# First layer of a decoder step on one core: the sample group's values stream past placed probabilities

## The chip, the cores and the metric

The kernel runs on one core of a Trainium2 chip. The metric is the device time of one execution in microseconds (us). The core has a matrix engine (TensorE, PE in the profile; its weight loads are shown apart as PEld), VectorE (DVE), ScalarE (ACT), GpSimd (POOL) and a queue that issues transfers (SyncE, SP). They run at the same time and meet only at semaphores. Matrix products are accumulated in PSUM, which has eight banks of 512 fp32 columns by 128 partitions.

## The reference

One inference step of a two-layer decoder, for a prompt of 512 tokens and for 8 sample sequences of one token each. This is the part that the change touches, cut from the function for the sample group in the first layer:

```python
def dilated_sample(q, k_new, v_new, k_buf, v_buf, rel_bias):
    ...
    for w, d in A_BRANCHES:                       # (128,1), (512,4), (2048,16)
        offs = branch_offsets(w, d)
        idx = wb + j[:, None] - offs[None, :]
        ...
        kg = jnp.where(in_buf, jnp.take(k_buf, ib, axis=1), jnp.take(k_new, inew, axis=1))
        vg = jnp.where(in_buf, jnp.take(v_buf, ib, axis=1), jnp.take(v_new, inew, axis=1))
        o, lse = gathered_attention(q, kg, vg, rel_bias_for(rel_bias, offs, h), (idx >= 0)[None])
    return combine_branches(outs, lses)
```

For each of 8 samples and 8 heads of 64 dimensions, a softmax over 256 cached keys and the new one, and the sum of the 257 value vectors weighted by it. The three branches are folded into one softmax with the logarithm of a count in the bias. Beside it the first layer has the same attention for the prompt, and a gated linear attention (GLA) with a state per sample; their joint result goes through an output projection and a SwiGLU block (called ffn below).

## The kernel before

Everything is fp32 at the borders. The large products are computed as three products of split operands (w_hi with act_hi, w_hi with act_lo, w_lo with act_hi), each of them 128x260 columns in fp32r (L701). ACT rounds a weight block to w_hi (`high`), POOL subtracts to get w_lo (`low`); two blocks are in flight. The input projection of the first layer has 25 such blocks (numbers 0 to 24); block n is written to one of two places in PSUM (banks 0 and 1 for even n, 2 and 3 for odd n) and moved out by ACT, which signals `free_a`. The last block is computed by `last_reader` (L880), which is done with chunks 4 to 7 of act_hi and act_lo first, so that staging for the attention can start in them.

The prompt attention of the first layer has 32 units (4 pairs of heads, 2 heads, 4 blocks of 128 queries, with 128, 256, 384 or 512 keys). It is a software pipeline whose order is written out by hand: step i issues on PE the scores of unit i (three fp32r products, L772), turns the probabilities of unit i-3 (L781) and adds the values of unit i-4 (L793); DVE adds the bias (L1761) and scales (L1769), ACT takes the exponential (L1374) and copies the turned probabilities (L1381). Scores go to banks 0 and 1, turned probabilities to 2 and 3, outputs to 4 and 5.

Behind each step a function `sample_a(i)` puts one piece of the sample group's work, in banks 6 and 7, on each engine's queue. On PE: GLA outputs of the samples (`sample_out_b`, step 0, 16 products of 2 columns, L1066), sum of squares for the last block's head norm (`last_head_sum`, step 1, L717), new values turned to rows (step 3, L1109; DVE copies them to `vnA` at step 4, L2015), norm sums of the GLA output (`norm_b`, 5 times from step 4, L1043), scores of the 8 samples (steps 5 to 15, L1078), probabilities turned (step 21, L1115), the new key's probability taken out (step 23, L1121), values of the 8 samples (steps 26 to 34, L1090) and the new value's share (step 35, L1126).

The values of one sample are 8 products: for each of 4 pairs of heads and 2 blocks of 128 keys, the cached values (128 keys by 128 dimensions) are the stationary operand and the probabilities of the two heads, two columns, move. The queries are laid out sparsely in `qzA` (2048 columns by 128 rows, mostly zero, in yA), which DVE clears (L2000) and fills (L2005) before its first unit. A plain fp32 product takes two records of the trace on PE.

## Time and profile before

| | us |
|---|---|
| median of 3 runs | 1583.71 |
| lowest and highest | 1576.1, 1595.62 |
| the profiled execution | 1597.1 |
| its span | 1595.3 |
| mean granted TensorE clock in it | 0.971 |

The rows further down are of the profiled execution; its span runs from the first to the last instruction, and 1.8 us of its time lie around that. "PEclk" is the share of TensorE's full clock that was granted: 1.00 is 2.4 GHz, 0.50 is 1.2 GHz, and there is nothing between.

### The profile page before, as it was taken

To read this page: it belongs to the slowest core of one execution; us is meant where nothing else is said; L and a number is where in the kernel's file an instruction comes from. 1 tells how busy PE (TensorE), PEld (TensorE's weight loads), DVE (VectorE), ACT (ScalarE), POOL (GpSimd) and SP (SyncE) were. 2 spreads that over 40 slices of the span, in tenths; PEclk is the share of its full clock that TensorE was granted. 3 is DMA by queue.
4 is the path that set the end of the run, shared out by engine and by line. 5 is a ranking of instruction groups with operands and counts; after the bars stand their busy time and mean duration, and the time that the engine had idled before them with its cause. 6 is when DMAs were issued, how large, how long until landed. Compare 5 with 4: busy or idle time off the path is not lost.

```text
span 1595.3 us, 31072 instructions
## 1 busy us (share of the span) xinstructions
PE 1537.8 (96%) x12240; PEld 1482.3 (93%) x12240; DVE 681.6 (43%) x1175; ACT 657.7 (41%) x1094; POOL 684.1 (43%) x350
## 2 busy tenths in 40 slices
PE   7999989999999999999989996999999999999998
PEld 6999967999999999999979785999999999999998
DVE  4044456145444343212341767775634443431224
ACT  4242646224433434222453554664344334332234
POOL 3654752033444444444336464221444444444444
PEclk9999979699999999999989997999999999999999
DMA  4222433122222323323223331121233332233333
GB/s 173 84 101 70 125 124 102 67 80 80 93 92 91 91 84 92 104 92 105 85 77 117 94 90 62 45 81 48 81 91 92 92 92 92 84 100 92 105 92 120
DMA packets 52837, 146.92 MB, mean 92 GB/s; under 512 B 5485, under 2 KB 18057, under 8 KB 52250
## 3 DMA queue, kind: packets, MB, share of 16 engines
q1 hardware_dynamic: 50346, 137.17, 27.7%
q10 hardware_dynamic: 2416, 8.72, 1.5%
q8 instruction: 50, 0.82, 0.2%
q14 instruction: 25, 0.20, 0.0%
HBM read 139.11 MB, written 6.76 MB: 91 GB/s over the span
## 4 chain that ended last, share of the span: by engine, by line
PE 89%; DVE 8%; ACT 2%; issue 1%; DMA 0%; SPq 0%; ACTq 0%; DVEq 0%
PE PS L701 70%; PE PS L793 4%; PE PS L772 3%; DVE act_lo L1741 2%; PE PS L781 2%; PE PS L1090 1%; PE PS L717 1%; PE PS L1078 1%; PE PS L770 1%; DVE top L2094 1%; PE PS L1156 1%; PE PS L1211 1%; DVE pp L1852 0%; DVE xC L2098 0%; PE PS L1066 0%
## 5 line engine op out<-in xcount | busy, mean ns | idle before, releaser
L494 POOL TENSOR_TENSOR w_lo<-w_raw,w_hi 128x1024 fp32r<-128x1024 f32 x217 | 534.9, 2465 | 802.9 <-ACT w_hi L1294 802.9
L701 PE MATMUL PS<-act_hi,w_hi 128*128 128x260 f32 x2576 | 739.4, 287 | 22.5 <-DVE act_lo L1741 12.5
L701 PE MATMUL PS<-act_lo,w_hi 128*128 128x260 f32 x2576 | 731.2, 284 | 0.0
L701 PE MATMUL PS<-act_hi,w_lo 128*128 128x260 f32 x2576 | 730.7, 284 | 0.0
L1294 ACT ACTIVATE w_hi<-w_raw 128x1024 fp32r<-128x1024 f32 x217 | 230.0, 1060 | 713.8 <-PE PS L701 710.0
L701 PEld LDWEIGHTS PS<-act_hi,w_hi 128*128 128x128 f32 x2576 | 488.0, 189 | 36.8 <-issue 23.6
L701 PEld LDWEIGHTS PS<-act_lo,w_hi 128*128 128x128 f32 x2576 | 488.7, 190 | 0.4
L701 PEld LDWEIGHTS PS<-act_hi,w_lo 128*128 128x128 f32 x2576 | 488.7, 190 | 0.0
L701 PE MATMUL PS<-h_hi,w_lo 128*128 128x260 f32 x704 | 198.8, 282 | 0.0
L701 PE MATMUL PS<-h_hi,w_hi 128*128 128x260 f32 x704 | 198.6, 282 | 0.0
L701 PE MATMUL PS<-h_lo,w_hi 128*128 128x260 f32 x704 | 198.5, 282 | 0.0
L701 PEld LDWEIGHTS PS<-h_hi,w_hi 128*128 128x128 f32 x704 | 132.6, 188 | 0.0
L701 PEld LDWEIGHTS PS<-h_lo,w_hi 128*128 128x128 f32 x704 | 132.3, 188 | 0.0
L701 PEld LDWEIGHTS PS<-h_hi,w_lo 128*128 128x128 f32 x704 | 132.2, 188 | 0.0
L1816 DVE TENSOR_TENSOR h_lo<-tmp,h_hi 128x520 f32 x44 | 84.0, 1908 | 40.1 <-ACT h_hi L1432 40.1
L1821 DVE TENSOR_TENSOR x<-PS,x 128x520 f32<-128x520 f32 x16 | 11.2, 699 | 176.5 <-PE PS L701 176.5
L1741 DVE SCALAR_TENSOR_TENSOR act_lo<-x,vecs,act_hi 128x520 fp32r<-128x520 f32 x48 | 70.8, 1494 | 23.2 <-ACT act_hi L1305 23.2
L1808 DVE TENSOR_TENSOR tmp<-PS,sq 128x520 f32<-128x520 f32 x44 | 30.8, 701 | 103.8 <-ACT sq L1428 103.8
L1812 DVE TENSOR_TENSOR tmp<-PS,tmp 128x520 f32<-128x520 f32 x44 | 30.8, 700 | 96.3 <-PE PS L701 96.3
L1381 ACT ACTIVATE tmp<-PS 128x128 f32<-128x128 f32 (+1 forms) x96 | 41.6, 433 | 71.1 <-PE PS L781 69.8
L1732 DVE TENSOR_TENSOR sqsum<-sqsum,sq 128x520 f32<-128x520 f32 x48 | 56.3, 1172 | 21.9 <-ACT sq L1300 21.1
L1806 DVE TENSOR_TENSOR tmp<-PS,nrs 128x520 f32<-128x520 f32 x44 | 30.8, 699 | 68.1 <-PE PS L701 68.1
(332 smaller groups left out, 1824.6 us busy)
## 6 DMA issues: line engine op xcount, KB each, us to landing
w_raw<-in_w SPq DMA_DIRECT2D x217, 512.0 KB, 3.5
kcA<-in_cache_k SPq DMA_DIRECT2D x8, 512.0 KB, 4.3
biasC<-scratch_rows SPq DMA_DIRECT2D x12, 256.0 KB
x<-in_xT SPq DMA_DIRECT2D x4, 520.0 KB, 5.9
out_y<-x SPq DMA_DIRECT2D x8, 260.0 KB, 4.5
vcA<-in_cache_v SPq DMA_DIRECT2D x4, 512.0 KB, 5.5
kcC<-in_pool_k SPq DMA_DIRECT2D x16, 128.0 KB, 2.5
vcC<-in_pool_v SPq DMA_DIRECT2D x16, 128.0 KB, 2.0
```

The costliest lines, as they stand in the source:

```text
L494: pool.tensor_tensor(w_lo[:, s, :], w_raw[:, s, :], w_hi[:, s, :].bitcast(F32), ALU.subtract).then_inc(S("w_lo"), 1)
L701: mm = pe.matmul(PS[:, 2 * place + half, 0:HALF], w[:, s, j * P:(j + 1) * P], r[:, c, cols], start=first and n == 0 and i == 0, stop=last ...
L772: mm = pe.matmul(PS[:, i % 2, 0:W], q_of[part][par][:, p % 2, qb * P:(qb + 1) * P], k[:, k_chunk(p), 0:W], start=n == 0 and not masked, st ...
L781: mm = pe.transpose(PS[:, 2 + i % 2, kb * P:(kb + 1) * P], ps[i % 3][:, kb * P:(kb + 1) * P], ident)
L793: mm = pe.matmul(PS[:, 4 + p % 2, qb * P:(qb + 1) * P], v_of(p, par, kb), pt[:, i % 2, kb * P:(kb + 1) * P], start=i % 8 == 0, stop=i % 8 ...
L1294: act.activation(w_hi[:, s, :], w_raw[:, s, :], ACT.Copy).then_inc(S("w_hi"), 1)
L1381: act.activation(pt[:, i % 2, 0:W], PS[:, 2 + i % 2, 0:W], ACT.Copy).then_inc(S("t_c"), 1)
L1732: dve.tensor_tensor(sqsum[:], sqsum[:], sq[:, m % 2, :], ALU.add).then_inc(S("ssum"), 1)
L1741: dve.scalar_tensor_tensor(act_lo[:, c, :], x[:, c, :], vecs[:, g:g + 1], act_hi[:, c, :].bitcast(F32), ALU.mult, ALU.subtract).then_inc(S ...
L1806: dve.tensor_tensor(halves(tmp[:, 1, :]), slot(0), halves(nrs[:]), ALU.mult).then_inc(S("f_a"), 1)
L1808: dve.tensor_tensor(halves(tmp[:, 1, :]), slot(0), halves(sq[:, 0, :]), ALU.mult).then_inc(S("free_v"), 1)
L1816: dve.tensor_tensor(h_lo[:, bass.ds(f, 1), :], tmp[:, 0:1, :], h_hi[:, bass.ds(f, 1), :].bitcast(F32), ALU.subtract).then_inc(S("h_lo"), 1)
```

## The change

Six edits, in the first layer only.

1. Values of a sample (`sample_values_a`): the turned probabilities are written by ACT into `pzA`, a field of zeros, so that for sample b and key block kb there is a stationary operand of 64 columns (one for each pair of head and sample) in which only the 8 columns of sample b are filled. The cached values of all heads (128 keys by 512) move. All 16 products accumulate in one bank, rows 0 to 63; a 17th product with the new keys' probabilities and values closes the sum. The result holds every head's row against every head's values; DVE copies it to `oA` (step 32), and four products with pieces of the identity (step 33) pick each head's own 64 dimensions and turn them to the layout that the output projection reads. The values stand at steps 24 to 31 instead of 26 to 34.
2. POOL clears `pzA` (128x1032) once the samples' scores are done; ACT waits for it at step 22.
3. DVE clears and fills `qzA` while the last input blocks are computed, before the first unit.
4. The first layer's scores use banks 2 and 3 and its turned probabilities banks 0 and 1, so that the first scores no longer wait for the last block to be moved out.
5. In the last input block ACT rounds the next weights behind the eviction instead of ahead of it, POOL adds the squares' term before its subtraction, and the transfer of the samples' state is issued before the key split. GLA outputs of the samples go half to step 0, half to step 1, the head sum to step 2; the new values are turned in bank 6, which `norm_b(0)` no longer waits for but the first sample scores do.
6. ACT and DVE split the samples' attention output straight from PSUM at the end of the stage, ahead of the last two GLA heads (`high_b`, `low_b` of 1 and 3).

```diff
-        VALUES_A = (26, 27, 28, 29, 30, 32, 33, 34)
+        VALUES_A = tuple(range(24, 32))
+        def score_bank(base, i):
+            return (2 if base == BASE_A else 0) + i % 2
+        def turned_bank(base, i):
+            return (0 if base == BASE_A else 2) + i % 2
...
+                if pair == 2:
+                    pool.wait_ge(S("s_ks"), NS)
+                    pool.memset(pzA, 0.0).then_inc(S("sm_pz"), 1)
...
             def norm_b(h):
                 pe.wait_ge(S("b_sq"), h + 1)
-                if h == 0:
-                    pe.wait_ge(S("sm_pnc"), 1)
-                else:
+                if h:
                     pe.wait_ge(S("b_ln"), h)
...
-            pe.wait_ge(S("free_a"), AB_BLOCKS + 2)
+            pe.wait_ge(S("free_a"), AB_BLOCKS + 1)
...
             def sample_values_a(b):
                 if b == 0:
+                    pe.wait_ge(S("sm_ptc"), 1)
+                    pe.wait_ge(S("b_ln"), 5)
+                pe.wait_ge(S(f"values{b % 6}"), 16 * (b // 6 + 1))
+                for kb in range(2):
+                    c = P * b + 64 * kb
+                    mm = pe.matmul(PS[0:64, 7, :], pzA[:, c:c + 64], value_place(b)[:, kb, :],
+                                   start=b == 0 and kb == 0, stop=False)
+                mm.then_inc(S("s_vs"), 1)
+                if b == NS - 1:
                     pe.wait_ge(S("sm_pnc"), 2)
-                pe.wait_ge(S(f"values{b % 6}"), 16 * (b // 6 + 1))
-                for t in range(4):
-                    for kb in range(2):
-                        c = t * NS + b
-                        mm = pe.matmul(PS[:, 7, 256 + 2 * c:258 + 2 * c], value_place(b)[:, kb, t * P:(t + 1) * P],
-                                       ptsA[:, kb, c:c + 33:32], start=kb == 0, stop=kb == 1)
-                mm.then_inc(S("s_vs"), 1)
+                    pe.matmul(PS[0:64, 7, :], pnA, vnA[:], start=False, stop=True).then_inc(S("sm_o"), 1)
...
-                elif i == 35:
-                    pn = pnA.rearrange("k (r t b) -> k r t b", r=2, t=4)
+                elif i == 33:
+                    pe.wait_ge(S("sm_oc"), 1)
                     for t in range(4):
-                        mm = pe.matmul(PS[:, 6, 16 * t:16 * t + 16], vnA[:, t * P:(t + 1) * P], pn[:, :, t, :],
+                        by_head = ident[0:64, 0:64].rearrange("k (r c) -> k r c", r=2)[:, :, NS * t:NS * t + NS]
+                        mm = pe.matmul(PS[:, 6, 256 + 16 * t:272 + 16 * t], oA[:, t * P:(t + 1) * P], by_head,
                                        start=True, stop=True)
...
                 elif i == 22:
                     act.wait_ge(S("sm_pt"), 1)
-                    act.activation(ptsA, PS[:, 7, 0:P].rearrange("p (n c) -> p n c", n=2),
+                    act.wait_ge(S("sm_pz"), 1)
+                    act.activation(pzA.rearrange("p (b m) -> p b m", b=NS)[:, :, 0:P:NS],
+                                   PS[:, 6, 0:P].rearrange("p (m b) -> p b m", b=NS),
                                    ACT.Copy).then_inc(S("sm_ptc"), 1)
...
             attention(PAIRS_A, BASE_A, xsA, psA3, statA, sample_a)
+            act.wait_ge(S("sm_o"), 2)
+            for r in range(2):
+                rows = slice(HD * r, HD * r + HD)
+                act.activation(act_hi[rows, 0:4, SEQ:NT], sample_out_a(r), ACT.Copy).then_inc(S("sm_oh"), 1)
             act.wait_ge(S("t_s"), 32)
             high_b(1)
             high_b(3)
-            act.wait_ge(S("sm_os"), 2)
-            act.activation(act_hi[:, 0:4, SEQ:NT], osA, ACT.Copy).then_inc(S("sm_oh"), 1)
```

On PE at steps 24 to 28, where the values of samples 0 to 2 stood before (vcA and s are places of cached values, nrs holds the turned probabilities):

```order
L772 MATMUL PS<-act_hi,q_hiA 128x384 [waits t_x]
...
L793 MATMUL PS<-tmp,rs 128x128 x2
L1090 MATMUL PS<-nrs,vcA 128x2 [waits values0,sm_pnc]
L1090 MATMUL PS<-nrs,vcA 128x2 x7
L772 MATMUL PS<-act_hi,q_hiA 128x512 [waits t_x]
...
L1090 MATMUL PS<-nrs,s 128x2 [waits values2]
L1090 MATMUL PS<-nrs,s 128x2 x7
```

And the same engine in the changed kernel, from step 24 and then at its end (yA holds pzA, sqsum the new values):

```order
L808 MATMUL PS<-tmp,rs 128x128 [waits A_st,A_zero,t_c]
L1103 MATMUL PS<-vcA,yA 64x512 [waits values0,b_ln,sm_ptc]
L1103 MATMUL PS<-vcA,yA 64x512
L787 MATMUL PS<-act_hi,q_hiA 128x256 [waits t_x]
...
L1103 MATMUL PS<-s,yA 64x512 [waits values1]
L1103 MATMUL PS<-s,yA 64x512
L1108 MATMUL PS<-sqsum,nrs 64x512 [waits sm_pnc]
...
L1143 MATMUL PS<-const,yA 128x16 [waits sm_oc]
L1143 MATMUL PS<-const,yA 128x16 x3
```

Eight products of 2 columns for each sample have become two of 512 columns, and they begin two steps earlier.

On PE behind the last input block, steps 0 to 5 before:

```order
L772 MATMUL PS<-act_hi,q_hiA 128x128 [waits k_split,A_st,t_x,A_zq,free_a]
...
L1066 MATMUL PS<-qz,s 128x2 [waits A_v,s_new,s_qz]
L1066 MATMUL PS<-qz,s 128x2 x15
...
L717 MATMUL PS<-sq,const 128x260 [waits n_rs,sq_e2,n_e2,hn_ln]
...
L1109 MATMUL PS<-const,yA 8x128 [waits b_o]
...
L1043 MATMUL PS<-s,const 128x512 [waits sm_pnc,b_sq]
...
L1074 MATMUL PS<-sbA 64x257 [waits sm_qz,sm_bias]
```

And now:

```order
L787 MATMUL PS<-act_hi,q_hiA 128x128 [waits k_split,A_st,t_x,A_zq,free_a]
...
L1078 MATMUL PS<-qz,s 128x2 x7
L787 MATMUL PS<-act_hi,q_hiA 128x256 [waits t_x]
...
L1078 MATMUL PS<-qz,s 128x2 x7
...
L732 MATMUL PS<-sq,const 128x260 [waits n_rs,sq_e2,n_e2,hn_ln]
...
L1126 MATMUL PS<-const,yA 8x128 x4
...
L1056 MATMUL PS<-s,const 128x512 [waits b_sq]
...
L1087 MATMUL PS<-sbA 64x257 [waits sm_pnc,sm_qz,sm_bias]
```

The GLA outputs (qz,s) are cut in two with the second unit's scores between them, and the wait for the copy of the new values (sm_pnc) has gone from the norm sum (L1043 before, L1056 now) to the first product of the sample scores.

On ACT around the eviction of the last input block, before:

```order
L1294 ACTIVATE w_hi<-w_raw 128x1024 [waits w_used,w_raw0]
L1533 ACTIVATE q_loA<-const 64x1024 [waits s_kv]
L1545 ACTIVATE act_hi<-yA 128x2x512 [waits act_free,hn_ok]
L1347 ACTIVATE yA<-PS,gains 128x520 [waits w_used]
L1348 ACTIVATE sq<-PS 128x520
L1330 ACTIVATE rs<-PS,vecs 128x520 [waits hn_ok,hn_ss]
```

And now:

```order
L1554 ACTIVATE q_loA<-const 64x1024 [waits s_kv]
L1565 DMA out_s_state<-s 128x2048 [waits s_new]
L1568 ACTIVATE act_hi<-yA 128x2x512 [waits act_free,hn_ok]
L1366 ACTIVATE yA<-PS,gains 128x520 [waits w_used]
L1367 ACTIVATE sq<-PS 128x520
L1311 ACTIVATE w_hi<-w_raw 128x1024 [waits w_used,w_raw0]
```

The rounding of the next weights (w_hi) has moved from the front of this row of work to behind the eviction, and the state's transfer to the front.

## Rows read from the trace of the kernel before

**Rows 1.** The page: busy time of the engines, and the chain that ended last.

```profile
PE 1537.8 (96%) x12240; PEld 1482.3 (93%) x12240; DVE 681.6 (43%) x1175; ACT 657.7 (41%) x1094; POOL 684.1 (43%) x350
...
PE 89%; DVE 8%; ACT 2%; issue 1%; DMA 0%; SPq 0%; ACTq 0%; DVEq 0%
PE PS L701 70%; PE PS L793 4%; PE PS L772 3%; DVE act_lo L1741 2%; PE PS L781 2%; PE PS L1090 1%; PE PS L717 1%; PE PS L1078 1%; PE PS L770 1%; DVE top L2094 1%; PE PS L1156 1%; PE PS L1211 1%; DVE pp L1852 0%; DVE xC L2098 0%; PE PS L1066 0%
```

**Rows 2.** Windows from the last input block to the ffn; PEclk is the granted clock.

```profile
core 0: us, PE busy (x) PEld busy (x) DVE busy (x) ACT busy (x) POOL busy (x), PEclk, DMA share, GB/s
202.00:205.20 3.20, 1.36 (x9) 0.84 (x8) 2.56 (x4) 3.17 (x5) 3.14 (x2) 1.00 0.00 0
205.40:218.80 13.40, 13.19 (x52) 11.99 (x53) 7.68 (x17) 6.14 (x13) 6.08 (x7) 0.50 0.31 117
219.00:222.20 3.20, 0.94 (x9) 0.75 (x7) 3.13 (x9) 1.79 (x7) 3.06 (x5) 1.00 0.21 86
222.50:225.60 3.10, 2.96 (x8) 1.96 (x9) 0.23 (x1) 0.00 (x0) 1.95 (x3) 0.50 0.55 220
225.90:270.00 44.10, 42.30 (x248) 30.81 (x247) 27.63 (x75) 24.94 (x73) 14.68 (x16) 1.00 0.46 144
270.30:273.40 3.10, 3.10 (x14) 3.00 (x14) 1.90 (x10) 1.58 (x4) 0.00 (x0) 0.50 0.02 5
273.70:287.00 13.30, 13.30 (x112) 12.69 (x111) 6.56 (x26) 7.09 (x22) 0.00 (x0) 1.00 0.24 77
287.30:324.60 37.30, 37.30 (x171) 36.55 (x170) 7.96 (x24) 6.71 (x17) 0.00 (x0) 0.50 0.12 43
324.90:340.00 15.10, 15.10 (x128) 15.10 (x127) 6.60 (x5) 3.36 (x5) 4.81 (x2) 1.00 0.27 88
```

**Rows 3.** Windows, PE alone: steps 24 to 35 at either clock.

```profile
core 0: us, PE busy (x), PEclk, DMA share, GB/s
275.50:287.10 11.60, 11.60 (x101) 1.00 0.29 91
287.10:320.10 33.00, 33.00 (x152) 0.50 0.14 49
```

**Rows 4.** Timeline of PE, the value products at either clock, and the end.

```profile
279.11 1.84 PE L1090 MATMUL PS<-nrs,vcA 128*128 128x2 f32 x16
280.82 0.48 PE L772 MATMUL PS<-act_hi,q_hiA 128*128 128x512 f32 x1
...
288.82 3.41 PE L1090 MATMUL PS<-nrs,kcA 128*128 128x2 f32 x16
292.09 0.67 PE L772 MATMUL PS<-act_hi 128*128 128x384 f32 x1
...
318.29 1.89 PE L1126 MATMUL PS<-nrs,sqsum 8*128 8x16 f32 x8
320.10 0.59 PE L701 MATMUL PS<-act_hi,w_hi 128*128 128x260 f32 x1
```

**Rows 5.** Timeline of PE at the full clock: fp32 products of 257 and 512 columns.

```profile
244.63 1.95 PE L1078 MATMUL PS<-kcA,yA 128*64 128x257 f32 x8
246.52 1.12 PE L1043 MATMUL PS<-s,const 128*128 128x512 f32 x2
247.08 0.63 PE L772 MATMUL PS<-act_hi 128*128 128x128 f32 x1
```

**Rows 6.** Timeline of all engines, steps 0 and 1.

```profile
202.62 1.06 ACT L1545 ACTIVATE act_hi<-yA 128x1024 fp32r<-128x1024 f32 x1
...
203.71 1.40 DVE L1965 TENSOR_TENSOR act_lo<-yA,act_hi 128x1024 fp32r<-128x1024 f32 x1 [0.64 <-ACT act_hi L1545]
...
205.03 1.27 DVE L1968 COPY vtokA<-PS 128x512 f32<-128x512 f32 x2
...
205.36 0.44 PE L772 MATMUL PS<-act_hi,q_hiA 128*128 128x128 f32 x1 [1.58 <-DVE act_lo L1965]
...
206.45 6.96 PE L1066 MATMUL PS<-qz,s 128*128 128x2 f32 x32 [0.21 <-DVE vtokA L1968]
206.68 1.76 DVE L2000 MEMSET yA<- 128x2048 f32 x1 [0.38 <-issue]
...
208.48 1.91 DVE L2005 COPY yA<-yA 64x32 f32<-64x32 f32 x2
...
210.43 0.29 DVE L1761 CUSTOM_DVE_ANT_0 xA<-PS,biasA 128x128 f32<-128x128 f32 x1
```

**Rows 7.** Timeline of PE, step 4: the wait ahead of the first norm sum.

```profile
222.64 2.05 PE L1043 MATMUL PS<-s,const 128*128 128x512 f32 x2 [2.70 <-DVE sqsum L2015]
...
226.31 0.64 PE L1074 MATMUL PS<-sbA 33*64 33x257 f32 x2
```

**Rows 8.** Timeline, step 21: the wait ahead of the turned sample probabilities.

```profile
269.93 0.34 PE L1115 MATMUL PS<-const,nrs 64*128 64x64 f32 x2 [1.33 <-DVE nrs L1862]
```

More of the change, by code:

```diff
@@ L539, in body @@
                         finish(n - 1, like - 1)
+                    q = normed(l, n, like)
+                    final = l == 0 and like == AB_BLOCKS - 1
+                    if final:
+                        add_eps(l, q, q % 2, n)
                     low(n + (b0 + 2), (b0 + like) % 2)
@@ L542, in body @@
                         after_low(like)
-                    q = normed(l, n, like)
-                    if q is not None:
+                    if q is not None and not final:
                         add_eps(l, q, q % 2, n)
@@ L1062, in sample_out_b @@
                 pe.wait_ge(S("A_v"), QB)
-                for i in range(2):
-                    for b in range(NS):
-                        c = 2 * (i * NS + b)
-                        mm = pe.matmul(PS[:, 7, c:c + 2], s0[:, b, i, :], qz8[:, i, b, :], start=True, stop=True)
+                for b in range(NS):
+                    c = 2 * (i * NS + b)
+                    mm = pe.matmul(PS[:, 7, c:c + 2], s0[:, b, i, :], qz8[:, i, b, :], start=True, stop=True)
                 mm.then_inc(S("s_o"), 1)
@@ L1335, in body @@
                 def body(n, like):
-                    high(n + (b0 + 2), (b0 + like) % 2)
+                    final = l == 0 and like == AB_BLOCKS - 1
+                    if not final:
+                        high(n + (b0 + 2), (b0 + like) % 2)
                     if before_evict:
@@ L1348, in body @@
                         act.activation(halves(sq[:, s, :]), place, ACT.Square).then_inc(S("free_a"), 1)
+                        if final:
+                            high(n + (b0 + 2), (b0 + like) % 2)
                     elif rank:
@@ L1947, in _ @@
             ins.then_inc(S("s_qz"), 1)
+            qz = qzA.rearrange("p m c -> p (m c)")
+            dve.wait_ge(S("s_qz"), 1)
+            then(dve.memset(qzA, 0.0))
             dve.wait_ge(S("s_in"), 16)
@@ L1960, in _ @@
                                   s0[:, b0:b0 + 4, i, :], ALU.add).then_inc(S("s_new"), 1)
+            dve.wait_ge(S("hn_ok"), 4 + 2)
+            for r in range(2):
+                rows = slice(HD * r, HD * r + HD)
+                dst = qz[rows, 32 * r:32 * r + 31 * 65 + 1:65].rearrange("p (t b) -> p t b", t=4)
+                dve.tensor_copy(dst, yA[rows, Y_Q:Y_Q + 4, SEQ:NT]).then_inc(S("sm_qz"), 1)
             dve.wait_ge(S("b_out"), 16)
@@ L1998, in bias_a @@
                 return biasA[:, p % 2, par, SEQ - W:SEQ]
-            qz = qzA.rearrange("p m c -> p (m c)")
-            then(dve.memset(qzA, 0.0))
-            dve.wait_ge(S("hn_ok"), 4 + 2)
-            for r in range(2):
-                rows = slice(HD * r, HD * r + HD)
-                dst = qz[rows, 32 * r:32 * r + 31 * 65 + 1:65].rearrange("p (t b) -> p t b", t=4)
-                dve.tensor_copy(dst, yA[rows, Y_Q:Y_Q + 4, SEQ:NT]).then_inc(S("sm_qz"), 1)
             def sample_a(i):
@@ L2027, in sample_a @@
                     low_b(2)
+                elif i == 32:
+                    dve.wait_ge(S("sm_o"), 1)
+                    dve.tensor_copy(oA, PS[0:64, 7, :]).then_inc(S("sm_oc"), 1)
             attention(PAIRS_A, BASE_A, xsA, psA3, statA, bias_a, sample_a)
+            for r in range(2):
+                rows = slice(HD * r, HD * r + HD)
+                dve.wait_ge(S("sm_oh"), r + 1)
+                dve.tensor_tensor(act_lo[rows, 0:4, SEQ:NT], sample_out_a(r), act_hi[rows, 0:4, SEQ:NT].bitcast(F32),
+                                  ALU.subtract).then_inc(S("a2_done"), 1)
             low_b(1)
             low_b(3)
-            dve.wait_ge(S("sm_o"), 1)
-            then(dve.tensor_copy(owA, PS[:, 6, 0:64].rearrange("p (t r b) -> p t r b", t=4, r=2)))
-            for r in range(2):
-                rows = slice(HD * r, HD * r + HD)
-                src = PS[rows, 7, 256:320].rearrange("p (t b r) -> p t b r", t=4, r=2)[:, :, :, r]
-                dve.tensor_tensor(osA[rows], src, owA[rows, :, r, :], ALU.add).then_inc(S("sm_os"), 1)
-            dve.wait_ge(S("sm_oh"), 1)
-            dve.tensor_tensor(act_lo[:, 0:4, SEQ:NT], osA, act_hi[:, 0:4, SEQ:NT].bitcast(F32),
-                              ALU.subtract).then_inc(S("a2_done"), 1)
-            dve.wait_ge(S("a2_done"), 1)
             ffn(0)
```

58 lines of the change are left out of this document (30 added, 28 removed).

## Prediction

> **What bounds the kernel now.** I read the page first: PE is busy for 96% of the span and carries 89% of the chain that ended last, most of it in the fp32r block products [rows 1]. So what the change is worth is PE time in the stage that it touches, and time on another engine counts only where PE waits for it. Then I read that stage in windows with the granted clock [rows 2]. The reader is to see that the stage is mostly not waiting but slow: from 205.4 to 218.8 us, from 222.5 to 225.6, from 270.3 to 273.4 and from 287.3 to 324.6 the clock is at 0.50 (1.2 GHz). Three of the falls stand behind idle time: PE was busy for 1.36 of 3.20 us before the first, 0.94 of 3.20 before the second, and had waited at step 21 before the third [rows 2, 7]. The fourth does not: PE was busy for all of 13.30 us before it. What ran there were the value products of the samples, whose moving operand has two columns; the engine was busy loading weights (PEld 12.69 of 13.30) and streamed next to nothing. The chain in order of time gives the price: 16 records of one sample take 1.68 us at the full clock and 3.21 us at half [rows 4]. Last I read the timeline at the start of the attention for who waits for whom [rows 5, 6].
>
> The profiled execution took 1597.1 us, 1.8 more than its span, and 13.4 more than the median of the runs. The working is made against it and carried to the median at the end.
>
> **The values, steps 24 to 35.** They take from 275.5 to 320.1 us: 11.6 us at full clock and 33.0 at half, with PE never idle [rows 3]. At the full clock the same instructions would take 11.6 + 33.0 / 2 = 28.1 us. Of this the eight samples' values are 8 x 1.68 = 13.4 us and the new value's share 1.81 / 2 = 0.9 us [rows 4], which leaves 13.8 us for the prompt's own work.
>
> Removed: the 13.4 + 0.9 us. Added: 16 products of 512 columns and the 17th for the new values. The trace has no such product with 64 columns stationary; it has two neighbours at the full clock. Four products of 257 columns with 64 stationary (the sample scores) take 1.88 us, 0.47 each, which scaled by 512/257 is 0.94 us. One product of 512 columns with 128 stationary (a norm sum) takes 1.06 us [rows 4]. I take 0.95, since the shape is that of the first: 17 x 0.95 = 16.2 us; by the dearer row it is 18.0. The four products that pick each head's part have the 8 records of the new value's share and its small moving operand: 0.9 us. Behind the values the last steps are a relay between PE and ACT: units 28 to 31 are turned, copied and added with nothing between, where before value products filled PE. I give that 1.0 us (the sum of two waits like the 1.33 at step 21 [rows 7] at most). Sum: 13.8 + 16.2 + 0.9 + 1.0 = 31.9 us at the full clock, against 28.1 before. **At equal clock the exchange is a loss of 3.8 us.** The gain is the clock: with 512 columns streaming in each product PE looks like it does from 225.9 to 270.0, where sample scores of 257 columns alternate with the same prompt work and the clock is 1.00 throughout [rows 2]. So 44.6 - 31.9 = 12.7 us are gained against this execution.
>
> The ffn's first block then starts at the full clock; up to 324.6 us it ran at half, 4.5 us of work that becomes 2.3. Its chunks of GLA heads 1 and 3 come late instead: ACT and DVE split them only behind the end of the attention, 1.15 and 1.30 us [rows 8], now also behind the small copies, and PE at double speed reaches them sooner. That is a wait of some 1.0 us. Net 1.3 us.
>
> Covers: ACT's copy into `pzA` is as long as the one that it replaces and PE takes it only at step 23; POOL's clearing of 1032 columns is about half of DVE's 2048 (1.76 us [rows 5]), at a time when it has nothing queued but the splits of the last pair, which PE needs 10 us later. The cached values come in ahead of use as before, since each step is longer than the old one at full clock. Nothing there costs.
>
> The Trainium skill (TensorE: Matmul & The Clock Gate, Back-to-back issue gap) has a pass of 512 columns at 216 ns warm. By it two records would be 0.43 us and the 17 products 7.3 us, and the gain would be 8.9 us more. The trace does not agree: 1.06 us for two records of 512 columns [rows 4].
>
> **The start, steps 0 to 5.** PE's first scores wait 1.58 us for DVE's key split, 203.71 to 205.11 [rows 5]. With ACT's rounding of the next weights out of the way the key split is bound only by DVE's two copies ahead of it and starts about 0.6 us earlier. PE then goes on when all four copies are in, before at 206.3, now about 0.65 us earlier. DVE's clearing and filling of `qzA`, 1.76 + 1.91 us, stood ahead of the first unit's bias at 210.43 but beside 6.96 us of GLA outputs on PE [rows 5]: moving it gains nothing by itself, and its new place is in DVE's idle time during the last blocks. Splitting the GLA outputs adds no work. At step 4 PE waits 2.70 us for the copy of the new values [rows 6]; the norm sum no longer needs it, only the square that ACT makes, which by my count of the queue is ready by then. The copy is now needed one unit and one norm sum later, about 3 us at half clock: I leave 0.5 us for it. With that idle time gone, the fall at 222.3 should not come, and 3.1 us at half clock [rows 2] become 1.6. Sum: 0.65 + 2.7 + 1.6 - 0.5 = 4.5 us. Bounds: 0, if the wait only moves to the first sample scores; and 8 us, if the clock does not fall at 205 either and half of the 6.96 us goes too.
>
> The step 21 wait [rows 7] hangs on DVE's softmax and stays, with its short fall of the clock.
>
> **From the profile to the median.** 12.7 + 1.3 + 4.5 = 18.5 us, which is 1578.6 us for an execution like the profiled one. The other runs of before were 1576.1 and 1583.7, so they may have kept the clock for longer. If an execution never lost it in the values, the change would gain 4.5 - 3.8 = 0.7 us there. I weigh the two ends two to one, 12.6 us, since every step from 26 to 34 has the same poor stream and a fall sooner or later is likelier than none. **1583.7 - 12.6 = 1571.1 us.**
>
> **Rivals.**
>
> *A, the clock was kept in the ordinary runs.* The long half-clock stretch is peculiar to the profiled execution, the slowest of all that are shown; for it speaks the 13.4 us between it and the median. Then the exchange of shapes nearly cancels the start: 1583.7 - 0.7 = 1583.0 us. Against it: nothing in the program makes one execution differ in what PE does before 287.
>
> *B, the start gains nothing.* The wait at step 4 moves to step 5, because ACT is held at step 1 by the head sum that now comes a step later on PE, and its square comes late. The values gain as forecast: 1571.1 + 4.5 = 1575.6 us.
>
> *C, slower: the clock falls all the same.* If fp32 products of 512 columns with 8 filled columns of 64, or the relay between them, do not hold the clock, all work behind the fall doubles. Falling at 287 as now, 11.5 us of the 31.9 are done and 20.4 become 40.8: 52.3 us against 44.6, a loss of 7.7, with no gain at the ffn and 4.5 at the start. Against the median that is 1583.7 + 3.2 = 1586.9, and 1591.4 without the start's gain. The point from which it decides: with the fall at f us after the start of the values the stage takes 63.8 - f, so it loses against 44.6 if f is under 19. For it speaks that the third neighbour, the norm sum, is rare; against it the whole stretch to 270.0. The Trainium skill (the same page, HAM oscillation) puts a fall down to idle gaps in PE. By it the fall at 287.2 with PE busy throughout would not be the doing of the value products, and this rival would gain weight; the row does not fit that rule, and I give it no more than below.
>
> *D, more than forecast.* The clock holds from 205 on as well: 1571.1 - 4 = 1567; and if a 512-column record comes cheaper, down to 1562.
>
> **Chances.** Forecast 0.60, A 0.12, B 0.13, C 0.07, D 0.08. The range reaches from D's far end to A's time and a little beyond for the spread of a median (the three runs lie 19.5 us apart): 1559 to 1585 us. Two per cent of 1583.7 is 31.7 us, about what a measurement of this kernel can tell from no change. No case reaches that far but together with a lucky or unlucky run: faster 0.05, same 0.94, slower 0.01.
>
> **What the profile after would show.** If the clock step is right, PEclk is 1.00 from step 22 to the ffn and beyond, the value records (2 for each product, 34 in all) end 0.45 to 0.53 us apart, and PE reaches the ffn some 32 us after step 24 began. If the start is right, the first norm sum shows no wait for DVE, and the sample scores begin 4 to 5 us earlier relative to the last input block. If the relay is right, PE has one or two waits for ACT's copies in the last four steps, of about 0.5 us each, and one for `act_lo` in the ffn's first block. Wrong would be: a half-clock stretch among the value products (C), or a profile before whose long stretch other executions lack (A, seen as after near 1583 with the clock at 1.00 in it).

## The result, and the profile after

| | before | after |
|---|---|---|
| median of 20 runs each, us | 1592.24 | 1582.54 |
| lowest and highest | 1576.10, 1598.84 | 1577.72, 1586.27 |
| the profiled execution | 1597.1 | 1580.17 |
| its span | 1595.3 | 1578.3 |
| mean granted TensorE clock in it | 0.971 | 0.981 |

After stands to before as 0.9945, with an interval from 0.9925 to 0.9966: faster by 5.4 to 11.9 us, 8.8 in the middle, which is inside the 2 per cent that the prediction called "same". Two repetitions at other times gave 0.9936 [0.9906, 0.9966] and 0.9934 [0.9902, 0.9966]. The time lies in the range that was forecast and is 11.4 us above the predicted one. The kernel before turned out slower than the median of the three runs that the prediction had: 1592.24 us instead of 1583.71.

Some of the prediction's references need a key, since the sections of its rows are numbered otherwise than it says. Its "rows 4" are the lengths in the chain of waits of before: 1.68 and 3.21 us for the 16 records of one sample's values at the two clocks, 1.88 for the sample scores, 1.06 for a norm sum, 1.81 for the new value's share. The timeline has the same instructions as 1.84, 3.41, 1.95, 1.12 and 1.89 us [rows 4, 5]. Its "rows 5" are [rows 6], its "rows 6" are [rows 7] and its "rows 7" are [rows 8]. Its "rows 8" (1.15 us on ACT and 1.30 on DVE at the end of the stage) stand in no group.

The page of the profile after, the lines that answer to [rows 1]:

```profile
PE 1522.4 (96%) x12146; PEld 1453.1 (92%) x12146; DVE 680.3 (43%) x1174; ACT 658.5 (42%) x1095; POOL 685.7 (43%) x351
...
PE 88%; DVE 8%; ACT 2%; issue 1%; DMA 0%; SPq 0%; ACTq 0%; DVEq 0%
```

PE still sets the time, with 15.4 us less of busy time. Windows of PE after, answering to [rows 2, 3]; the columns are the stretch and its length, PE's busy time and instructions, the granted clock, and the transfers:

```profile
core 0: us, PE busy (x), PEclk, DMA share, GB/s
200.19:206.81 6.62, 3.29 (x24) 0.98 0.00 0
206.81:224.13 17.32, 17.02 (x74) 0.61 0.19 72
224.13:268.04 43.91, 41.36 (x241) 1.00 0.50 153
268.04:274.87 6.83, 6.48 (x26) 0.50 0.00 1
275.37:308.06 32.69, 32.67 (x158) 1.00 0.24 81
```

The last row is the stage of the values, step 24 to the ffn: 32.69 us at the full clock, where before it took 44.60 [rows 3]. The row above it is new in size: the half clock around step 21 lasts 6.83 us instead of the 3.4 of before. Timeline of PE after, steps 24, 25 and the end of the stage, which answers to [rows 4]:

```profile
276.32 1.93 PE L1103 MATMUL PS<-vcA,yA 128*64 128x512 f32 x4
278.18 0.39 PE L787 MATMUL PS<-act_hi,q_hiA 128*128 128x256 f32 x1
...
302.26 1.07 PE L1108 MATMUL PS<-sqsum,nrs 8*64 8x512 f32 x2
303.25 0.44 PE L796 MATMUL PS<-const,sq 128*128 128x128 f32 x2
...
304.81 1.06 PE L1143 MATMUL PS<-const,yA 64*128 64x16 f32 x8
305.80 0.66 PE L796 MATMUL PS<-const,pA 128*128 128x128 f32 x4
...
308.06 0.37 PE L716 MATMUL PS<-act_hi,w_hi 128*128 128x260 f32 x1
```

A sample's two products hold PE for 1.86 us (276.32 to 278.18), 0.93 each. Timeline after at the start of the attention (POOL, DVE, PE), which answers to [rows 6]:

```profile
203.11 2.37 POOL L503 TENSOR_TENSOR w_lo<-w_raw,w_hi 128x1024 fp32r<-128x1024 f32 x1
203.21 3.34 DVE L1998 TENSOR_TENSOR act_lo<-yA,act_hi 128x1024 fp32r<-128x1024 f32 x1
...
205.54 1.49 POOL L586 CAST act_hi<-yA 64x512 fp32r<-64x512 f32 x1
...
206.81 0.45 PE L787 MATMUL PS<-act_hi,q_hiA 128*128 128x128 f32 x1 [2.92 <-DVE act_lo L1998]
```

DVE's key split began 0.5 us earlier than before but took 3.34 us instead of 1.40 [rows 6], so PE's first scores waited 2.92 us instead of 1.58 and began at 206.81 instead of 205.36. And after at steps 4 and 21, answering to [rows 7, 8]:

```profile
221.48 1.02 PE L1056 MATMUL PS<-s,const 128*128 128x512 f32 x2
...
268.39 0.47 PE L1131 MATMUL PS<-const,nrs 64*128 64x64 f32 x2 [1.33 <-DVE nrs L1887]
```

The wait of 2.70 us ahead of the first norm sum is gone; the one at step 21 is the same.

### The profile page after: what moved, and what is told of

Read it like the earlier page. It is cut to its first block, busy times and chain, and to the rows that moved or that the text cites. A ratio compares the mean times of both kernels' runs of the same rounds, so it can differ in the third digit from the quotient of the medians.

```text
span 1578.3 us, 30885 instructions
## 1 busy us (share of the span) xinstructions
PE 1522.4 (96%) x12146; PEld 1453.1 (92%) x12146; DVE 680.3 (43%) x1174; ACT 658.5 (42%) x1095; POOL 685.7 (43%) x351
## 4 chain that ended last, share of the span: by engine, by line
PE 88%; DVE 8%; ACT 2%; issue 1%; DMA 0%; SPq 0%; ACTq 0%; DVEq 0%
PE PS L716 71%; PE PS L808 3%; PE PS L787 3%; DVE act_lo L1766 2%; PE PS L796 2%; PE PS L732 1%; PE PS L1091 1%; PE PS L1103 1%; PE PS L785 1%; DVE top L2118 1%; PE PS L1173 1%; PE PS L1228 1%; DVE xC L2122 0%; PE PS L1078 0%; DVE tmp L1862 0%
## 5 line engine op out<-in xcount | busy, mean ns | idle before, releaser
L716 PE MATMUL PS<-act_hi,w_hi 128*128 128x260 f32 x2576 | 737.1, 286 | 22.7 <-DVE act_lo L1766 11.9
L716 PEld LDWEIGHTS PS<-act_hi,w_hi 128*128 128x128 f32 x2576 | 487.0, 189 | 38.2 <-issue 23.8
L1757 DVE TENSOR_TENSOR sqsum<-sqsum,sq 128x520 f32<-128x520 f32 x48 | 56.2, 1172 | 21.9 <-ACT sq L1317 21.2
```

Source lines behind the costliest of these rows:

```text
L716: mm = pe.matmul(PS[:, 2 * place + half, 0:HALF], w[:, s, j * P:(j + 1) * P], r[:, c, cols], start=first and n == 0 and i == 0, stop=last ...
L1757: dve.tensor_tensor(sqsum[:], sqsum[:], sq[:, m % 2, :], ALU.add).then_inc(S("ssum"), 1)
```

## The experiments

The stage lengths that the verdicts use are these, read from the trace of each run. The moment at which the last block ends varies by 1.6 us between executions, whatever the kernel, so the stages are counted from there (from the start of its last product). "Before, second" and "third" are the runs e5 and e12, "after, second" and "third" are e6 and e9.

| profile of | last block's end to first scores | to step 24 | step 24 to ffn | ffn to the end |
|---|---|---|---|---|
| before, first | 5.29 | 75.43 | 44.60 | 1275.2 |
| before, second | 5.29 | 75.55 | 31.46 | 1270.8 |
| before, third | 5.28 | 72.17 | 34.91 | 1273.1 |
| after, first | 6.62 | 75.18 | 32.69 | 1270.2 |
| after, second | 6.61 | 74.81 | 32.69 | 1271.8 |
| after, third | 6.60 | 73.67 | 32.70 | 1270.7 |
| e1, columns added to before | 5.29 | 75.55 | 40.33 | 1273.0 |
| e2, values alone | 5.28 | 77.84 | 32.70 | 1271.2 |
| e3, start alone | 6.61 | 72.41 | 44.82 | 1275.2 |
| e4 and e10, key split first | 4.50, 4.50 | 71.78, 72.05 | 32.68, 32.70 | 1269.2, 1275.2 |
| e7, columns at the start | 8.16 | 74.62 | 32.70 | 1272.4 |
| e8, columns at start and step 21 | 6.95 | 70.52 | 32.69 | 1272.6 |
| e11, columns at step 21 | 4.49 | 69.58 | 32.69 | 1272.0 |

### e1: does the stream of columns keep the clock?

```diff
                 mm.then_inc(S("s_vs"), 1)
+                if b == 0:
+                    pe.wait_ge(S("topk"), 1)
+                for _ in range(6):
+                    pe.matmul(PS[:, 6, :], identR[:], act_hi[:, 0, 0:SEQ], start=True, stop=True)
```

> The kernel before, with six products of 512 fp32r columns added behind the values of each of the 8 samples in steps 26 to 34. They write to a bank whose content is spent and nothing reads them, so the output stays the same and only work is added: 48 products, about 10.3 us at full clock by the 0.215 us of such a product in the ffn. Theory (it is the stream of operand columns that keeps the clock, and the old value products stream only 2 columns each): the granted clock stays at 1.00 through the values, the stage from step 24 to the ffn takes about 38 us instead of 44.6, and the kernel is 3 to 8 us faster than before although it does more. Rival 1 (the clock falls there for another cause, such as the work done in steps 19 to 23): the half-clock stretch stays and the kernel is 10 to 20 us slower. Rival 2 (executions without the profiler keep the clock there anyway, the profile shows it lower): the profile shows a shorter stage but the timed runs are about 10 us slower.

Measured: 1588.34 us (1584.86 to 1591.38, 12 runs) against 1594.12 for before (34 runs), ratio 0.9977 [0.9950, 1.0005]. Window of e1 from step 24 to the ffn, and its added products on the timeline:

```profile
275.86:316.19 40.33, 40.33 (x300) 1.00 0.20 66
```

```profile
279.48 1.84 PE L1090 MATMUL PS<-nrs,vcA 128*128 128x2 f32 x16
281.18 1.65 PE L1096 MATMUL PS<-act_hi,identR 128*128 128x512 f32 x6
```

With 48 products added that nothing reads, the clock stays at 1.00 through the whole stage, which is 4.3 us shorter than that of the first profile of before (though longer than the 31.46 and 34.91 us of the other two, in which the half clock was short). A product in a row of six took 0.25 us (281.18 to 282.67) and not the 0.215 of the expectation, so the stage takes 40.3 us and not 38. The timed runs agree on the clock: the mean granted clock is 0.982 to 0.985 in all 12 of e1, and 0.969 to 0.982 in the runs of before for which it is on record. That the time as a whole is shorter too the interval does not quite show. The old value products, the idle time and the work ahead of them are all unchanged here, so rival 1 is out: it is the thin stream behind the 2-column products that loses the clock. It is not the share of time spent on loading weights: PEld is busy for 37.49 of the 40.33 us of e1, nearly as much as in before (12.69 of 13.30) [rows 2]. Rival 2 expected times 10 us above before, and is out as well.

The prediction had set this against the Trainium skill (TensorE: Matmul & The Clock Gate, HAM oscillation), which puts a fall down to gaps in which PE is idle. The row and this run settle it for this kernel: PE was busy for all of 13.30 us ahead of the long fall in before [rows 2], and adding columns without removing any gap kept the clock.

### e2 and e3: the values alone, the start alone

e2 is the changed kernel with edits 3, 4 and 5 put back, of which three:

```diff
-            return (2 if base == BASE_A else 0) + i % 2
+            return i % 2
...
-                if h:
+                if h == 0:
+                    pe.wait_ge(S("sm_pnc"), 1)
+                else:
...
-                    final = l == 0 and like == AB_BLOCKS - 1
+                    final = False
```

> The changed kernel with its start put back as it was: banks of scores and turned probabilities, the first norm sum behind the copy of the new values, the GLA outputs of the samples all in step 0, the head sum in step 1, the place of clearing and filling qzA, the order of ACT and POOL in the last input block, the state's transfer. Only the new form of the values and the relay behind it stay. Theory (all of the gain is in the values and the ffn's start): as fast as the changed kernel within 2 us, 7 to 11 us faster than before; the DVE key split takes 1.4 us again and the first scores wait 1.6 us. Rival (the start gave what it was forecast to give, 4.5 us, and the values less): 4 to 5 us slower than the changed kernel.

e3 is the kernel before with edits 3, 4 and 5 made in it and the old value products kept, of which three:

```diff
+            return (2 if base == BASE_A else 0) + i % 2
...
-                if h == 0:
-                    pe.wait_ge(S("sm_pnc"), 1)
-                else:
+                if h:
...
+                    final = l == 0 and like == AB_BLOCKS - 1
+                    if final:
+                        add_eps(l, q, q % 2, n)
```

> The kernel before with only the edits of the start and the last input block (edits 3, 4 and 5), and the old value products. Theory (the start gains 2.7 us by the first sample scores and loses them to the waits and the longer half clock around steps 19 to 21): within 2 us of the kernel before, the half-clock stretch in the values as before. Rival (the start gains): 3 to 5 us faster than before. Rival (the slower key split and the added waits cost): 1 to 3 us slower.

Measured: e2 1583.35 us (12 runs), 0.9951 [0.9920, 0.9981] of before; e3 1589.23 us (12 runs), 0.9975 [0.9942, 1.0008]. Windows of e3, then of e2:

```profile
272.62:284.06 11.44, 11.44 (x100) 1.00 0.27 89
284.06:317.44 33.38, 33.38 (x153) 0.50 0.14 49
```

```profile
277.94:310.64 32.70, 32.68 (x158) 1.00 0.23 81
270.32:277.15 6.83, 5.93 (x23) 0.50 0.00 1
```

The new values alone give the changed kernel's stage (32.70 us) and nearly its whole gain; the start alone keeps the long half-clock stretch and cannot be told from before. In e3's profile step 24 comes 3.0 us sooner after the last block than in the first profile of before, but the third profile of before has the same (72.17 against 72.41) without any edit. So a gain of the start of up to 3 us stays possible in single executions, and the timed runs show none.

The two runs also tell where the changed kernel loses that gain again. From the first sample score to step 24 the five profiles with the old values take 48.5 to 48.7 us (the three of before, e1, e3), the seven with the new ones and no products added there 49.8 to 51.2 (after, e6, e9, e2, e4, e10, e7), e2 with the old start among them. So the loss goes with the values and not with the start. POOL, DVE and PE behind the sample scores, after:

```profile
256.19 0.96 POOL L656 MEMSET yA<- 128x1032 f32 x1 [13.74 <-PE PS L1091]
...
261.98 1.60 POOL L591 TENSOR_TENSOR act_lo<-yA,act_hi 64x512 fp32r<-64x512 f32 x1
...
262.48 1.65 DVE L2024 TENSOR_TENSOR yA<-yA 128x512 f32<-128x512 f32 x1
...
264.79 0.39 PE L787 MATMUL PS<-act_hi 128*128 128x256 f32 x1 [0.77 <-DVE statA L1786]
```

The same in e3:

```profile
258.77 1.40 POOL L588 TENSOR_TENSOR act_lo<-yA,act_hi 64x512 fp32r<-64x512 f32 x1
...
262.21 0.69 DVE L2011 TENSOR_TENSOR yA<-yA 128x512 f32<-128x512 f32 x1
```

POOL holds back its clearing of `pzA` (edit 2) until the sample scores are done and waits 13.74 us for them, and its splits for the last pair of heads come behind it. They begin 33.0 us after the first sample score instead of 29.2 in before (257.10 - 224.13, 256.10 - 226.88). One of them now runs beside DVE's gate of the GLA output, which takes 1.65 us instead of 0.69; DVE is late with the next unit, and PE waits 0.77 us where e3 and before have no wait. The long DVE row stands at this place in all nine profiles with the new values and in none of the five with the old ones. No run took the clearing away, so its part is read from the traces and not shown by an experiment.

DVE and POOL in e2, with the old order of the last block:

```profile
201.68 2.36 POOL L503 TENSOR_TENSOR w_lo<-w_raw,w_hi 128x1024 fp32r<-128x1024 f32 x1 [1.99 <-ACT w_hi L1315]
204.10 1.49 POOL L586 CAST act_hi<-yA 64x512 fp32r<-64x512 f32 x1
```

```profile
203.73 1.39 DVE L1994 TENSOR_TENSOR act_lo<-yA,act_hi 128x1024 fp32r<-128x1024 f32 x1 [0.64 <-ACT act_hi L1570]
```

There the subtraction of POOL was nearly over (204.04) when the key split began, and the split took 1.39 us.

### e4 and e10: the key split ahead of POOL's subtraction

```diff
                         add_eps(l, q, q % 2, n)
+                        pool.wait_ge(S("k_split"), 1)
                     low(n + (b0 + 2), (b0 + like) % 2)
```

> The changed kernel with one wait added: POOL subtracts for the low part of the last block's weights only after DVE's split of the keys. Theory (the key split takes 3.34 us instead of 1.40 because POOL's subtraction of 2.4 us runs beside it): the key split takes 1.4 us again, the first scores start about 1.9 us earlier; whether that reaches the end is open, 0 to 2 us faster than the changed kernel. Rival (the split is long because its own operands or its place changed, not because of POOL): it stays at 3.3 us, the last block waits longer for its low part, and the kernel is 1 to 2 us slower than the changed one.

> The changed kernel with the key split ahead of POOL's subtraction, once more, now beside the changed kernel itself. Theory (the slow key split costs 1.5 to 2 us that reach the end): 1.5 to 4 us faster than the changed kernel. Rival (the earlier 1578.34 against 1582.54 was the difference of two chips or sessions, and the gain is swallowed by a later wait): within 1 us.

Measured: e4 1578.34 us (11 runs), 0.9926 [0.9897, 0.9955] of before. e10, the same kernel: 1577.10 us (9 runs), 0.9899 [0.9867, 0.9931]. Beside it ran the changed kernel:

> The changed kernel once more, as the yardstick for the next two on the same chip: 1580 to 1582.5 us.

It took 1579.25 us (12 runs), 0.9934 [0.9902, 0.9966], so the wait gains 2.2 us by the medians; the intervals overlap. e4's median was 4.2 us below that of the changed kernel's first 20 runs (1578.34 against 1582.54), which ran apart from it. Both point the same way, and the size is uncertain. DVE, POOL and PE in e4:

```profile
204.57 1.23 DVE L1999 TENSOR_TENSOR act_lo<-yA,act_hi 128x1024 fp32r<-128x1024 f32 x1
```

```profile
205.87 2.37 POOL L503 TENSOR_TENSOR w_lo<-w_raw,w_hi 128x1024 fp32r<-128x1024 f32 x1 [1.35 <-DVE act_lo L1999]
208.30 0.61 POOL L587 CAST act_hi<-yA 64x512 fp32r<-64x512 f32 x1
```

```profile
206.05 0.30 PE L788 MATMUL PS<-act_hi,q_hiA 128*128 128x128 f32 x1 [0.80 <-DVE act_lo L1999]
```

The key split falls from 3.34 to 1.23 us and the first scores come 2.1 us sooner after the last block (4.50 against 6.62), in both profiles. The cause of the slow split is shown: it is the neighbour on POOL, not the split's operands or place. The times on the three timelines fit a lock that the first comer holds to its end. In after POOL is done at 205.48 and DVE 1.07 us later; in e2 POOL is done at 204.04 and DVE 1.08 us later; and POOL's cast, 0.61 us alone in e4, takes 1.49 us in e2, where it starts 1.02 us before DVE is done. DVE's gate of the GLA output (see e2 and e3) has the same form: it ends 0.55 us behind POOL's split, at 264.13 and 263.58, and takes 0.69 us alone.

This is a rule of the Trainium skill (SBUF — State Buffer, SBUF: two separate sides): a VectorE operation with two SBUF inputs and a GpSimd operation that reads SBUF take a shared pair of ports in turn, and the later one is fully blocked. The traces agree, with the numbers just given. The prediction did not weigh it, though it is the rule that spoke against edit 5.

### e5 and e12: the kernel before, profiled again

No edit.

> The kernel before, unchanged, for a second profile of it; together with the one time it shows whether every execution loses the clock in the values. Theory (the fall there is a property of the program, only its length and place vary): half clock again among the value products of steps 26 to 34, a time near 1594 us if it is as long as in the first profile. Rival A of the prediction (ordinary executions keep it): values at 1.00 throughout, ffn some 10 to 14 us earlier, a time near 1578 us.

> The kernel before, unchanged, for a third profile. The two profiles so far lose the clock in the values at 287.2 and at 303.4 us, with times of 1597.1 and 1581.2 us. Theory (the moment of the fall differs between executions and with it the time, step 24 to the ffn taking 28.8 us plus what lies behind the fall): the time follows the fall here too, about 1597 - 11 x (fraction of the stage ahead of the fall beyond the first profile's), between 1577 and 1598 us. Rival (the spread of the times comes from elsewhere, such as the second layer): the fall lies anywhere and the time does not follow it.

Measured: 1581.19 and 1581.99 us. Windows of e5, then of e12 (its whole stage, and the two stretches at half clock, of which the second reaches 4.5 us past the stage's end):

```profile
277.16:303.38 26.22, 26.22 (x229) 1.00 0.29 102
303.38:308.62 5.24, 5.24 (x24) 0.50 0.00 0
```

```profile
272.15:307.06 34.91, 34.91 (x252) 0.82 0.22 76
284.30:291.10 6.80, 6.80 (x33) 0.50 0.65 233
301.40:311.60 10.20, 10.20 (x47) 0.50 0.00 0
```

The same instructions took 44.6, 31.5 and 34.9 us in three executions, by where the clock fell and how soon it came back. It fell in each of them, so rival A's "kept" is too strong, but in two of three the fall was short or late. e12 also corrects the theory that was stated for it: the fall came early, at 284.3, and the time was low all the same, since the clock came back at 291.1. The length counts, not only the moment.

The timed runs show the same spread. In all, before had 104 runs: 61 above 1590 us, with a mean of 1595.4, and 43 below, with a mean of 1583.4. The line at 1590 is drawn by hand, and some times lie close to it on both sides. The changed kernel had 44 runs, none above 1586.3, with a mean of 1580.9. The mean granted clock is on record for 84 of the 104: it is 0.969 to 0.973 in every run above 1590 us and 0.975 to 0.982 in every run below. The group means, 0.971 and 0.979, differ by 0.008, which on 1595 us is some 12 us (an estimate), as much as the times differ. So it is the clock that sets the two groups apart. That it fell in the values, and not elsewhere, is an inference from the three profiles, in which the 1597.1 us go with the long fall and the 1581 to 1582 with the short ones.

### e6: the changed kernel again

No edit.

> The changed kernel, unchanged, beside the next two on the same chip. About 1582.5 us as before. Its second profile also shows whether the short pace of the blocks in the last ffn (mean 282 ns for a product, 496.5 us from its start to the end) belongs to the program or to the one execution: 496.5 again, or 498.5 to 498.9 as in the four others profiled so far.

Measured: 1579.77 us (12 runs), 0.9936 of before. The last ffn, from its first block to the end, in the first profile of after and then in e6:

```profile
1081.75:1578.26 496.51, 484.73 (x4043) 1.00 0.30 94
```

```profile
1081.34:1580.84 499.50, 487.93 (x4043) 0.99 0.30 94
```

The 2 us that the first profile of after had gained here belong to the execution, not to the program: e5 and e12, the kernel before, took 496.5 there as well. e6 also has 3.4 us at half clock in that stretch. What makes the rest of the difference stays open.

### e7, e8 and e11: columns against the other falls

e8 has all of this edit; e7 lacks the lines of steps 19 and 21, e11 the lines of the start. All three have the wait of e4.

```diff
+            def stream(n):
+                for _ in range(n):
+                    pe.matmul(PS[:, 6, :], identR[:], act_hi[:, 0, 0:SEQ], start=True, stop=True)
+
+            pe.wait_ge(S("A_v"), QB - 1)
+            stream(8)
...
                     mm = pe.matmul(PS[:, 7, c:c + 2], s0[:, b, i, :], qz8[:, i, b, :], start=True, stop=True)
+                    stream(1)
...
+                elif i == 19:
+                    pe.wait_ge(S("s_e"), 1)
+                    stream(3)
...
                 elif i == 21:
+                    stream(6)
                     pe.wait_ge(S("sm_sx"), 2)
```

> The kernel with the key split first, and products added that nothing reads: 8 of 512 fp32r columns while PE waits for the key split ahead of the first scores, and one behind each of the 16 GLA outputs of the samples in steps 0 and 1. Full-clock price by rows: the first 8 lie partly in a wait of 0.8 us (8 x 0.215 = 1.7 us), the other 16 cost at most 3.4 us. Theory (a poor stream of columns is what loses the clock at the start too): no half-clock stretch of 13.65 us at step 0; the two groups of GLA outputs take 2 to 3.5 us each instead of 3.5, all prompt work up to step 4 runs at full clock, and the sample scores start 1 to 5 us earlier than in the kernel without the added products. Rival (the fall at the start has another cause, such as the idle times just ahead of the first scores): half clock all the same, and 3 to 7 us slower.

> The kernel of the run before, with 9 more such products: 3 at the end of step 19 and 6 ahead of the turned probabilities of step 21, where PE waits 0.8, 0.5 and 1.3 us. Price at full clock 1.9 us, most of it inside these waits. Theory: the half-clock stretch of 3.4 to 6.8 us around step 21 goes, 1 to 3 us gained. Rival: it stays, and the products only add 0 to 2 us.

> The kernel of the run before with the 9 added products around steps 19 to 21 only, and none at the start. Theory (the fall of the clock around step 21 comes from the 2.6 us of waits there, the added columns prevent it and lie mostly in these waits): no half-clock stretch there, 1 to 2 us faster than without them, and the half clock at step 0 stays at 10 to 14 us. Rival: the gain of the version with both came from the start alone, and this one is no faster.

Measured: e7 1579.96 us (12 runs), 0.9939 [0.9908, 0.9969] of before; e8 1577.58 (12 runs), 0.9927 [0.9896, 0.9957]; e11 1575.79 (7 runs, 1574.95 to 1577.10), 0.9897 [0.9860, 0.9934]. Windows of e7, e8 and e11:

```profile
203.00:206.87 3.87, 2.16 (x15) 1.00 0.00 0
206.87:210.29 3.42, 3.42 (x12) 0.50 0.00 0
210.29:225.21 14.92, 13.92 (x88) 1.00 0.22 85
```

```profile
200.40:270.90 70.50, 66.99 (x400) 1.00 0.36 113
```

```profile
206.10:216.30 10.20, 10.20 (x42) 0.50 0.00 0
216.30:269.60 53.30, 51.91 (x306) 1.00 0.47 150
```

In e8 the clock stays at 1.00 from the last block to the ffn, in e7 the stretch of 10 to 14 us at the start shrinks to 3.4, and in e11 the one around step 21 is gone. So every fall of the first layer yields to added columns. At the start it pays nothing: from the last block to the first sample score PE needs 23.8 us in e7 and 21.2 to 21.9 without the added work (e4, e10, e11), and e7's time is no better than the changed kernel's 1579.77, measured beside it. The gain in clock was spent on the 24 products, and the first eight, with the wait for DVE's copies that was put ahead of them, put off the first scores by 3.7 us (8.16 against 4.50). Around step 21 it pays: the nine products lie mostly in waits, and step 24 comes at 69.58 us instead of 71.78 and 72.05. Counted from the first sample score, where the luck of the start is left out, it is 48.2 us against 49.8 and 50.9. e11 beats before, and also the changed kernel (1579.25; 10 of its 12 runs lie above the slowest of e11). By its median it is 1.3 us below e10 (1577.10) as well, with 7 and 9 runs, which is not a clear difference.

## Why the prediction was right and wrong

**The exchange of shapes** was right, also in its sign. In the full-clock equivalent the old stage takes 26.22 + 5.24 / 2 = 28.8 us by e5 (28.1 forecast), and the new one takes 32.7 in all its profiles (31.9 forecast): a loss of 3.9 us against the 3.8 predicted. Inside it the 17 products took 8 x 1.86 + 0.99 = 15.9 us (16.2 forecast) and the picking of heads 0.99 (0.9). The relay has no wait in the last four steps; the prompt's own work takes 32.7 - 15.9 - 1.0 = 15.8 us, 2.0 above the 13.8 that it was given, and that took the relay's place. So the sum was right within 0.8 us partly by luck. The wait in the ffn's first block came as forecast, if shorter: 0.66 us in one row. One sign was only half met: PEclk was to be 1.00 from step 22 on, and the half clock around step 21 lasted until step 24 nearly began (274.87 of 275.37).

**The clock in the values** was right as a mechanism, and against the profiled execution as a size: 44.6 - 32.7 = 11.9 us, with 12.7 forecast. e1 shows the cause directly.

**The start** was wrong: 4.5 us forecast, and by step 24 only 0.25 us are left against the first profile (75.43 to 75.18). Two steps of the prediction failed.

The first is the term "0.65 for an earlier key split". It was in truth a loss of 1.33 us (6.62 against 5.29), because edit 5 brings POOL's subtraction and DVE's split together; e4 gives back 2.1 us. The other terms went about as forecast: the wait at the norm sum is gone, and the clock does not fall there in any profile that lacks the wait. (It does not fall there in e12 either, which has a wait of 1.68 us, so the fall is not certain in before.) The first sample score came 2.9 us sooner after the last block (23.94 against 26.81), not 4 to 5.

The second is "Nothing there costs", said of POOL's clearing of `pzA`. The clearing itself is as short as forecast, 0.96 us. But between the first sample score and step 24 the changed kernel lost 2.6 us again. Half clock around step 21 lasted 6.83 us in two of three profiles of after and 3.4 in all three of before, which is 1.7 us of them; the other 0.9 go with the waits that the late splits on POOL bring (see e2 and e3). The prediction placed the clearing by its length and the free time on POOL, and did not look at which engine would run beside what was pushed back. The fall of 6.83 us stands in five of the seven profiles with new values and no products added there, and in none of the five with old ones; that these waits cause it too is likely and not shown.

Rival B, the start gains nothing, is near to what happened, but by other mechanisms than the one it named. The step 21 wait "stays" was right, its clock not: its fall was longer, and e11 shows some 2 us to be had there.

**From the profile to the median** is the step that put the predicted time off most. For the two ends it forecast a gain of 18.5 us against an execution with the long fall and 0.7 without. Measured were 1597.1 - 1580.2 = 16.9 us and, for e5 and e12 against the changed kernel's mean of 1580.9, 0.2 to 1.0 us. By the means of the two groups it is 14.5 and 2.4 us. So the ends were near. The weights of two to one were near the 61 to 43 of the timed runs, but they were laid on the median of three runs, 1583.71, which belonged to the lower group. The third of these runs, 1595.62 us, the prediction used only for its range ("19.5 us apart"); in the weighing it named 1576.1 and 1583.7 as "the other runs". With it two of the four known executions were near 1596, which spoke against rival A as well. With the median of 20 the same 12.6 us would have given 1579.6. So of the 11.4 us by which 1571.1 was too low, 8.5 are the base and 2.9 the gain (9.7 between the medians instead of 12.6), and these 2.9 are fewer than the 4.5 us of the start that did not come. That the time still lies in the range is the width of the range, not the working. The prediction even saw the sign of the trouble, 13.4 us between the profiled execution and the median, and should have used it: the median and an execution of the other group are not to be mixed.

Rival A is half right, as an account of 43 runs in 104. C did not occur: PEclk is 1.00 among the value products in every profile that has the new ones. D did not occur.

## What to carry to other kernels

Where PE is busy throughout and still at half clock, look at how many columns its products stream; here products of 2 columns lost the clock and those of 512 kept it, and a form that costs 3.9 us more at equal clock can be the faster and the steadier one. When an execution can fall into a long slow stretch, take the base of a forecast from many runs or from the group that the profile belongs to, and forecast the spread: here the groups of before lay 14.5 and 2.4 us above the changed kernel. Before moving a VectorE operation with two SBUF inputs, look at what GpSimd reads at that moment; and before giving GpSimd a new wait, look at what its work behind that wait will then run beside.

## What was not expected of the hardware

The half clock around step 21 can be taken away with products that nothing reads, at no cost that shows where they lie in waits (e11). The fall among value products came 11.6 to 26.2 us after step 24 began, and lasted from 6.8 to 37.6 us, in executions of the same program. The last ffn, the same instructions at the full clock, ran in 496.5 or 498.5 us from one execution to the next, by products of 282 or 283 ns; no cause was found.
